# A hybrid gMLP and stick-breaking trunk on one core: gated product in the `up` bank, mixing one tile sooner, normalisation between the accumulations of `down`

## The reference

```
z = gelu(x @ w_in); u, v = split(z)              # 2048 columns each
v = layer_norm(v, v_g, v_b)                      # over the 2048 columns
v -> (8 chunks of 128 positions, 8 groups of 256 columns)
mixed = einsum('gts,bcsgd->bctgd', tril(w_s), v) + b_s
out = (u * mixed) @ w_out
```

## Time and profile before

| | |
|---|---|
| median of 3 executions | 2876.8 us (2876.49 to 2879.41) |
| the profiled execution | 2878.36 us, span of its instructions 2876.6 us |
| mean granted clock of TensorE | 0.966 of full speed |
| PE busy, span | 2661.8 us, 93% |
| DVE busy | 1357.7 us, 47% |
| ACT busy | 856.6 us, 30% |
| POOL busy | 780.0 us, 27% |

### The profile page before, as it was taken

One profiled execution on the slowest core, in us unless ns is written; L12 is line 12 of the kernel. 1 busy time (PEld: TensorE's weight loads), 2 busy tenths in 40 slices (PEclk: granted clock), 3 DMA queues, 4 the chain that ended last, 5 costly groups with the idle time before them and its releaser, 6 DMA issues.

```text
span 2876.6 us, 37135 instructions
## 1 busy us (share of the span) xinstructions
PE 2661.8 (93%) x13772; PEld 2274.0 (79%) x13772; DVE 1357.7 (47%) x1801; ACT 856.6 (30%) x1307; POOL 780.0 (27%) x372
## 2 busy tenths in 40 slices
PE   7998998999999999999999976667899999999998
PEld 7997777777888888887988765556787888888886
DVE  3216666665333343346211298888444333343344
ACT  4222121143211211114212266666333211211112
POOL 2112112222121121123212255554331121121122
PEclk9999999999999999999999988888999999999999
DMA  4222121142111111123334633332122111111123
GB/s 154 88 88 103 44 74 59 44 147 74 44 50 53 44 44 58 44 87 110 125 132 156 209 82 87 88 88 66 51 88 82 45 48 55 44 44 58 44 80 103
DMA packets 113297, 228.70 MB, mean 80 GB/s; under 512 B 9664, under 2 KB 76224, under 8 KB 111168
## 3 DMA queue, kind: packets, MB, share of 16 engines
q1 hardware_dynamic: 105408, 194.02, 21.9%
q10 hardware_dynamic: 7808, 33.56, 2.9%
HBM read 177.23 MB, written 50.33 MB: 79 GB/s over the span
## 4 chain that ended last, share of the span: by engine, by line
issue 54%; PE 22%; POOL 12%; DVE 9%; ACT 2%; DMA 1%; DVEq 0%; POOLq 0%; ACTq 0%; SPq 0%
POOL w_lo L511 10%; PE psum L584 8%; PE psum L595 5%; DVE stick L1423 3%; PE psum L571 3%; PE psum L814 2%; DVE vst L1276 2%; POOL brk L545 2%; DVE aT_lo L1429 1%; PE psum L673 1%; PE psum L828 1%; POOL xt L526 1%; PE psum L797 1%; DVE vn_lo L1285 1%; ACT vn_hi L1004 1%
## 5 line engine op out<-in xcount | busy, mean ns | idle before, releaser
L511 POOL TENSOR_TENSOR w_lo<-stage,w_hi 128x1024 fp32r<-128x1024 f32 x208 | 500.6, 2428 | 1817.0 <-ACT w_hi L883 1817.0
L571 PE MATMUL psum<-hT_hi,w_hi 128*128 128x512 f32 x1536 | 599.3, 390 | 2.0 <-POOL w_lo L511 2.0
L571 PE MATMUL psum<-hT_lo,w_hi 128*128 128x512 f32 x1536 | 598.7, 390 | 0.0
L571 PE MATMUL psum<-hT_hi,w_lo 128*128 128x512 f32 x1536 | 598.3, 389 | 0.0
L595 PE MATMUL psum<-w_hi,a_hi 128*128 128x512 f32 x1280 | 504.7, 394 | 25.9 <-DVE acc L1270 16.6
L1270 DVE TENSOR_TENSOR acc<-psum,acc 128x512 f32<-128x512 f32 x544 | 373.5, 690 | 317.7 <-PE psum L595 314.0
L595 PE MATMUL psum<-w_lo,a_hi 128*128 128x512 f32 x1280 | 502.8, 393 | 0.0
L595 PE MATMUL psum<-w_hi,a_lo 128*128 128x512 f32 x1280 | 502.2, 392 | 0.0
L883 ACT ACTIVATE w_hi<-stage 128x2048 fp32r<-128x2048 f32 x104 | 198.6, 1909 | 737.6 <-PE psum L595 663.4
L1345 DVE TENSOR_TENSOR psum<-psum,relu 128x512 f32<-128x512 f32 x128 | 89.6, 700 | 535.8 <-ACT relu L1050 535.8
L571 PEld LDWEIGHTS psum<-hT_hi,w_hi 128*128 128x128 f32 x1536 | 289.0, 188 | 62.0 <-issue 2.0
(11 more groups left out here) (95 smaller groups left out, 2936.6 us busy)
## 6 DMA issues: line engine op xcount, KB each, us to landing
stage<-mlp_w_in SPq DMA_DIRECT2D x64, 1024.0 KB, 5.3
stage<-a_w_in_in SPq DMA_DIRECT2D x16, 1024.0 KB, 5.5
x_res<-xt SPq DMA_DIRECT2D x24, 512.0 KB, 4.6
xt<-x_res SPq DMA_DIRECT2D x24, 512.0 KB, 5.3
stage<-b_w_qkv_in SPq DMA_DIRECT2D x12, 1024.0 KB, 5.1
xt<-x_in SPq DMA_DIRECT2D x16, 512.0 KB, 4.3
v_gelu<-vring ACTq DMA_DIRECT2D x8, 1024.0 KB, 3.9
vst<-v_gelu SPq DMA_DIRECT2D x8, 1024.0 KB, 4.8
```

What stands on the lines that cost most here:

```text
L511: pool.tensor_tensor(wt[b][1][:, c], stage[:, c], wt[b][0][:, c].bitcast(F32), ALU.subtract).then_inc(unit_ready, 1)
L571: mm = pe.matmul(psum[:, bank, :], wt[ub][sw][:, k * UC + f * P:k * UC + (f + 1) * P], hT[sh][:, k, half * HALF:(half + 1) * HALF], start= ...
```

## The change

It has three parts:

- The gated product is written into `psum[:, j]`, the bank of tile j of `up`, instead of `ut`. `a_hi` and `a_lo` read it from there. So tile j of `up` waits, in the gMLP stage too, until `a_lo` j of the chunk before is done.
- Mixing items 2 and 3 are issued behind tile 2 (except in the first chunk, which stays). `vn_hi` and `vn_lo` are made in two halves by token tiles 0 to 3 and 4 to 7; items 0 and 1 wait for the first, items 2 and 3 for the second.
- The normalisations of the chunk after next are put one by one behind accumulations 1 to 8 of `down`, the two halves of `vn_lo` behind 11 and 13, and `bb` behind 15. The last `a_lo` of the upper chunk comes behind accumulation 0. ACT makes `vn_hi` after the `w_hi` of the `up` unit; for the last chunk that `w_hi` comes behind gelu 3. Chunks 0 and 1 have their values made outside of `down`. SP's load of `vst` waits for both halves of the last `vn_lo`.

```diff
--- before.py
+++ after.py
@@ -365,7 +365,7 @@
 
                 def load_v(c):
 
-                    wait(sp, vn_lo, c)
+                    wait(sp, vn_lo, c * 2)
                     if isinstance(c, int) and c == 0:
                         for b in range(2):
                             wait(sp, v_out[b], 16 * AW // UC // 2)
@@ -664,8 +664,8 @@
 
                     half, f = j // 2, j % 2
                     bi = mix_item(c) + j
-                    if j == 0:
-                        pe.wait_ge(vn_lo, c + 1)
+                    if f == 0:
+                        pe.wait_ge(vn_lo, c * 2 + (half + 1))
                     pe.wait_ge(back_evac, bi - 1)
                     for t in range(4 * half, 4 * half + 4):
                         bank, c0 = 4 + 2 * (j % 2) + (t % 4) // 2, (t % 2) * 2 * P
@@ -685,13 +685,12 @@
                             pe.wait_ge(hT_done, HB * (norm + 1))
                         for f in range(2):
                             j = 2 * half + f
-                            if not mix:
-                                wait(pe, ch_lo, c * 4 + (ai0 + j - 3))
+                            wait(pe, ch_lo, c * 4 + (ai0 + j - 3))
                             t_item((act_evac, 0) if mix else None, c * 4 + (fi0 + j), j, 0 if first else 1, f, half,
                                    u0 if first and norm is not None and j == 0 else None).then_inc(front_psum, 1)
                             if mix:
 
-                                for item in (((), (), (0, 1), (2, 3)) if first else ((), (0, 1), (2,), (3,)))[j]:
+                                for item in (((), (), (0, 1), (2, 3)) if first else ((), (0, 1), (2, 3), ()))[j]:
                                     mixing(c, item)
                             if first and norm is not None and j == 0:
 
@@ -994,14 +993,19 @@
             hi(U_A + 1, 1)
 
 
+            def values_hi(c, half):
+
+                act.wait_ge(vn_nat, c * 2 + (half + 1))
+                if not (isinstance(c, int) and c == 0):
+                    act.wait_ge(back_psum, mix_item(c - 1) + 4)
+                act.activation(vn[0][:, 4 * half:4 * half + 4, :], vst[:, 4 * half:4 * half + 4, :],
+                               ACT.Copy).then_inc(vn_hi, 1)
+
             def gate_chunk(c, ab):
-                if not (isinstance(c, int) and c == 0):
+                first, last = isinstance(c, int) and c == 0, isinstance(c, int) and c == CH_A - 1
+                if not first:
                     act.wait_ge(back_psum, s_end(c - 2, BI_A, 20, 8))
                     hi(c * 2 + U_A, 0)
-                wait(act, vn_nat, c + 1)
-                if not (isinstance(c, int) and c == 0):
-                    act.wait_ge(back_psum, mix_item(c - 1) + 4)
-                act.activation(vn[0][:], vst[:], ACT.Copy).then_inc(vn_hi, 1)
 
                 def gelu(j):
                     act.wait_ge(front_psum, c * 4 + (FI_A + j + 1))
@@ -1011,23 +1015,27 @@
                 def gated_hi(j):
                     act.wait_ge(back_evac, mix_item(c) + (j + 1))
                     act.wait_ge(back_psum, s_end(c - 2, BI_A, 20, 8))
-                    act.activation(a_buf[ab][0][:, j % 2, (j // 2) * HALF:(j // 2 + 1) * HALF], ut[:, j, :],
+                    act.activation(a_buf[ab][0][:, j % 2, (j // 2) * HALF:(j // 2 + 1) * HALF], psum[:, j, :],
                                    ACT.Copy).then_inc(ch_hi, 1)
 
                 gelu(0)
                 gelu(1)
                 gated_hi(0)
+                gated_hi(1)
                 gelu(2)
-                gated_hi(1)
-                last = isinstance(c, int) and c == CH_A - 1
+                gated_hi(2)
+                gelu(3)
                 if last:
-                    act.wait_ge(front_psum, FI_A + 4 * CH_A)
-                    hi(c * 2 + (U_A + 1), 1)
-                gelu(3)
-                gated_hi(2)
-                if not last and not (isinstance(c, int) and c == 0):
                     hi(c * 2 + (U_A + 1), 1)
                 gated_hi(3)
+                if not last and not first:
+                    hi(c * 2 + (U_A + 1), 1)
+                if not last:
+                    values_hi(c + 1, 0)
+                    values_hi(c + 1, 1)
+
+            values_hi(0, 0)
+            values_hi(0, 1)
 
             def gate_step(i):
                 if isinstance(i, int) and i == 0:
@@ -1270,61 +1278,109 @@
                 return dve.tensor_tensor(dst, src, dst, ALU.add)
 
 
-            def gate_chunk(c, ab):
-                dve.wait_ge(v_in, c * 16 + 16)
-                for t in range(NT):
-                    ins = dve.tensor_scalar(vst[:, t, :], vst[:, t, :], mv[:, t, 0:1], v_rs[:, t:t + 1],
-                                            ALU.subtract, ALU.mult)
-                ins.then_inc(vn_nat, 1)
+            def normed(c, t):
+
+                if t == 0:
+                    dve.wait_ge(v_in, c * 16 + 16)
+                ins = dve.tensor_scalar(vst[:, t, :], vst[:, t, :], mv[:, t, 0:1], v_rs[:, t:t + 1],
+                                        ALU.subtract, ALU.mult)
+                if t % 4 == 3:
+                    ins.then_inc(vn_nat, 1)
+
+            def values_lo(c, half):
+
+                dve.wait_ge(vn_hi, c * 2 + (half + 1))
+                dst = (slice(None), slice(4 * half, 4 * half + 4), slice(None))
+                dve.tensor_tensor(vn[1][dst], vst[dst], vn[0][dst].bitcast(F32), ALU.subtract).then_inc(vn_lo, 1)
+
+            def bias(c):
 
                 wait(dve, gate, c * 8)
                 for f in range(2):
                     dve.scalar_tensor_tensor(bb[:, f, :], rs_bc[:, bass.ds(c * P, P)], vb_c[:, bass.ds(c * 2 + f, 1)],
                                              bs_bc[:, bass.ds(c * P, P)], ALU.mult, ALU.add).then_inc(bb_set, 1)
-                dve.wait_ge(vn_hi, c + 1)
-                dve.tensor_tensor(vn[1][:], vst[:], vn[0][:].bitcast(F32), ALU.subtract).then_inc(vn_lo, 1)
-                dve.wait_ge(bb_set, c * 2 + 2)
-
-                def gated_lo(j):
-                    dve.wait_ge(ch_hi, c * 4 + (j + 1))
...
-                    dve.tensor_tensor(a_buf[ab][1][dst], ut[:, j, :], a_buf[ab][0][dst].bitcast(F32),
-                                      ALU.subtract).then_inc(ch_lo, 1)
-
-                for j in range(4):
...
-                    dve.wait_ge(back_psum, bi + 1)
-                    dve.wait_ge(act_evac, c * 4 + (FI_A + j + 1))
...
-                    dve.tensor_tensor(u, mixed[:, :, 0], u, ALU.mult).then_inc(back_evac, 1)
-                    if j:
-                        gated_lo(j - 1)
-                gated_lo(3)
+
+            def affine(c, j):
+
+                f = j % 2
+                dve.wait_ge(back_psum, mix_item(c) + (j + 1))
+                if j == 0:
+                    dve.wait_ge(bb_set, c * 2 + 2)
+                mixed = psum[:, 4 + 2 * f:6 + 2 * f, :].rearrange("p a (t s n) -> p (a t) s n", t=2, s=2)
+                v_gain = vg_c[:, bass.ds(c * 2 + f, 1)]
+                dve.scalar_tensor_tensor(mix_lo[:], mixed[:, :, 1], v_gain,
+                                         bb[:, f:f + 1, :].to_broadcast([P, 4, P]), ALU.mult, ALU.add).then_inc(gate, 1)
+                dve.wait_ge(gate, c * 8 + (2 * j + 1))
+                dve.scalar_tensor_tensor(mixed[:, :, 0], mixed[:, :, 0], v_gain, mix_lo[:],
+                                         ALU.mult, ALU.add).then_inc(gate, 1)
+
+            def gated(c, j):
+
+                f = j % 2
+                mixed = psum[:, 4 + 2 * f:6 + 2 * f, :].rearrange("p a (t s n) -> p (a t) s n", t=2, s=2)
+                dve.wait_ge(gate, c * 8 + (2 * j + 2))
+                dve.wait_ge(act_evac, c * 4 + (FI_A + j + 1))
+                dve.tensor_tensor(psum[:, j, :].rearrange("p (t n) -> p t n", t=4), mixed[:, :, 0],
+                                  ut[:, j, :].rearrange("p (t n) -> p t n", t=4), ALU.mult).then_inc(back_evac, 1)
+
+            def gated_lo(c, ab, j):
+
+                dve.wait_ge(ch_hi, c * 4 + (j + 1))
+                dst = (slice(None), j % 2, slice((j // 2) * HALF, (j // 2 + 1) * HALF))
+                dve.tensor_tensor(a_buf[ab][1][dst], psum[:, j, :], a_buf[ab][0][dst].bitcast(F32),
+                                  ALU.subtract).then_inc(ch_lo, 1)
+
+            def gate_chunk(c, ab):
+                for j in range(2):
+                    affine(c, j)
+                    gated(c, j)
+                gated_lo(c, ab, 0)
+                gated_lo(c, ab, 1)
+                affine(c, 2)
+                gated(c, 2)
+                affine(c, 3)
+                gated_lo(c, ab, 2)
+                gated(c, 3)
+
+            def values(c):
+                for t in range(NT):
+                    normed(c, t)
+                bias(c)
+                for half in range(2):
+                    values_lo(c, half)
 
             def s_part(c, bi0, per, extra, copy):
                 for j in range(16):
```

(47 more changed lines are left out.)

## The result

| | before | changed |
|---|---|---|
| median | 2877.25 us (2876.49 to 2879.41, 4 runs) | 2831.26 us (2829.17 to 2831.53, 4 runs) |
| span of the profiled execution | 2876.6 us | 2829.5 us |

The ratio is 0.9837, with a 95% interval of 0.9825 to 0.985: 46 us gained.

What follows compares the result with a forecast made beforehand. TensorE was taken to bound the gMLP stage, with gaps before the mixing and at the fifth piece of `down`. Gains of 41.7 - 0.4 + 3.4 = 44.7 us gave a forecast of 2833 us, range 2828 to 2843.

Steps and rivals of the forecast that it cites:

- The gap at the fifth piece of `down`: TensorE waits for `acc` because GpSimd's `w_lo` holds two `a_lo`; six waits, 17.8 us, were to go.
- The wait for `vn_lo`: TensorE waits before the mixing, eight times, 13.0 us; normalisations between accumulations of `down` were to close it.
- DVE's row in `down`: Layout of accumulations and normalisations, two held: accumulation 3 at T + 7.6, 4 at T + 10.1, least slack 0.8 us.
- T: The end of tile 3 of `up`, from which the prediction counts its times in `down` and the tail.
- The signs: What the profile after would show, among it two normalisations of about 2.5 us in each `down`.
- Rival B: DVE falls behind in `down` as more normalisations are held: 2853 to 2860 us, or 2841 with one more; chance 0.15.
- The rule for at most one SBUF input: Such a DVE instruction doesn't contend with GpSimd, so `a_lo` reading PSUM was priced at 0.69 us, not held.
- the stage: The gMLP chunks, 215 to 602 us: waits, restarts behind 14 gaps and half-clock stretches, together 41.7 us gained.
- the tail: Last unit of the gMLP: a new 2.1 us gap for `w_lo` where 1.7 were, 0.4 us lost.
- the boundary: Behind the tail: sooner loads shrink DVE's wait for the gain from 4.3 to about 1; 3.4 us gained, bounds 0 and 4.

Runs made afterwards that it cites:

- e1: The kernel before with only part 1, the gated product in the bank of `up`, mixing and normalisation order as before: 2848.86 us.
- e2: The changed kernel with part 1 undone: the product stays in `ut`, and `a_hi` and `a_lo` read it from SBUF: 2831.98 us.
- e5: The changed kernel with all eight normalisations, bias and `vn_lo` behind the last accumulation of `down` instead of between accumulations: 2831.48 us.
- e10: As e5, but ACT makes `w_hi` of the `down` unit first and `vn_hi` after it, so `w_lo` runs beside the normalisations: 2835.21 us.
- e6: The changed kernel with each normalisation cut in four instructions of 64 columns: 2852.85 us.
- e3: The kernel before with mixing item 3 issued behind tile 2 instead of tile 3, nothing else: 2863.96 us.
- e8: The changed kernel with the old mixing order, item 3 again behind tile 3: 2833.64 us.
- e7: The changed kernel with SP loading x and the boundary's gains after the last mixing item instead of after the last `a_lo`: 2830.53 us.
- e9: The changed kernel with the sooner loads of e7 and, in the last chunk, ACT's `w_hi` ahead of gelu 3: 2829.17 us.

## Why the prediction was right, and where it was off

**The gap at the fifth piece of `down`.** Cause and size were right: 17.8 us of waits went, and e1 took away the same by the cause alone. What the prediction did not say is that parts 1 and 2 with the new ACT order each suffice (e1, e2). A sum by parts would have counted it twice; the forecast summed by gaps.

**The wait for `vn_lo`.** The forecast that it goes was right. The reason given, normalisations in the shadow of `down`, was sufficient but not necessary: e5 has them behind `down` and e10 even beside `w_lo`, at the same period. In chunks 2 to 7 the halves are enough (e10); chunk 1 also needs `vn_hi` ahead of `w_hi` (e5 has no wait there, e10 one of 2.9 us).

**DVE's row in `down`.** Laid out: accumulation 3 at T + 7.6 and 4 at T + 10.1; measured 7.2 and 9.6, with two of eight held. The signs named two normalisations of about 2.5 us; they took 1.6 to 1.9, as in the layout itself, because they begin 0.7 to 0.9 us into a `w_lo`. Rival B did not come. The least slack was 1.3 us, at accumulation 4, and e6, with 0.6 us more for each normalisation and one of them held twice, went over the edge. The Trainium skill, SBUF — State Buffer, § Who interferes with whom, says that a DVE instruction with two SBUF inputs contends with a GpSimd instruction that reads SBUF, over a port pair that is locked and not shared. The traces agree: 2.70 us for a subtraction of 0.68 begun 0.6 us into a `w_lo` (e3), and none of the 32 with a PSUM operand above 0.70 (e1). The rule for at most one SBUF input, which the prediction draws on, is given there only outside the two-port modes; the normalisations, which read one tile from SBUF and not two, were held before and after the change.

**The mis-sized terms.** First, the stage gained 43.6 us, where 41.7 were summed. A gap costs more than its length: the first matmul behind it holds up the next by 0.34 us instead of 0.23 (e8), and the first one of the mixing by 0.22 instead of 0.11. By their starts 16 mixing matmuls behind a wait took 2.01 us where the changed kernel has 1.91 (of the 0.26 us by which the 2.17 of the earlier trace rows are longer, 0.16 are already in the sum). That makes 0.1 us for each of 14 gaps, 1.5 us. The other 0.4 us is 0.06 us per chunk: without its waits, the short period of the kernel before would be 47.46 us, not 47.40. Second, the tail lost 0.2 instead of 0.4 us. Third, the boundary gained 1.7 instead of 3.4. Up to the first tile of the MLP it gained 3.3, as summed (from the first piece of chunk 7, 45.8 us instead of 49.1): the wait for the gain shrank to 0.94 as laid out, and the gap with its half-clock stretch at 614 went. But a half-clock stretch now follows at the end of the boundary and takes 1.6 us back; the sum has no term for it. Its cause is open. The 1.5 us wait of the transposes ahead of it is the same in all traces; seven have the stretch behind it (both of the changed kernel, e3, e5, e7, e8, e10), and five don't (before, e1, e2, e6, e9), though TensorE's waits from chunk 7 to there are alike within 0.1 us in e6 and the changed kernel.

**The rest**, 1.9 us, lies before and behind the stages that changed; the start of `up` and the time behind the boundary scatter by as much between traces. That the forecast came within 1.7 us is in part luck: the stage gave 1.9 us more than summed, the boundary 1.7 less, and the two cancel.

## What to carry to other kernels

Where one engine bounds a stage, sum the gaps of that engine, with what follows each (the clock, the restart), and not the parts of the change: several parts can cure the same gap. Before you move work into another's shadow, look whether something simpler closes the same gap: here two halves did in six chunks, and with the order of two ACT instructions in chunk 1 too, and the move added nothing. When an engine's row is interleaved with one that frees buffers, lay it out piece by piece; the sum of busy times (17.8 of 21.8 us) did not show an edge that was 1.3 us away.

## What the runs showed of the hardware

- A DVE subtraction with two SBUF operands, begun while GpSimd subtracts in SBUF, ended 0.55 us after GpSimd's instruction did, and a held normalisation 0.15 us after: the subtraction took 2.5 to 2.8 us instead of 0.68 (21 held ones in the kernel before, e2 and e3), the normalisation 1.6 to 2.6 instead of 0.41 where it began in the first 0.9 us. One PSUM operand removes this (e1). GpSimd pays too: a `w_lo` that began while such a subtraction was running took 2.8 us instead of 2.4 (the second of each pair in the kernel before, both in e3, where the pair took 5.55 us instead of 4.8). Two `w_lo` in a row held two DVE instructions, however short these were: in four `down` of e6 four parts of one normalisation met both `w_lo` and took 5.22 us, so that cutting finer made the accumulation behind them later.
- Behind every wait inside `down` at full clock, from 0.1 us (e8) to 3.0 us (before), TensorE's first matmul took 0.34 us to the next one instead of 0.23.
- TensorE's granted clock fell to half after four of six gaps of 3.0 us and after the one of 5.7, and not after the six of 1.0 us in e3 or the six of 0.9 to 1.3 us ahead of the mixing in e1. The length of the gap alone does not decide it: one of 2.3 us in the tail of e2 had a stretch at half clock behind it and one of 2.3 us in e3 had none, one of 1.8 us had one in the boundary of the kernel before and none in the tail of the changed kernel, and one of 2.9 us in e10 had none.
